# Gate and up as seven half-size block products, down in one pass per third, in a two-layer decoder kernel

## What is computed

```
def finish(x, m, w_o, g_post_mix, g_pre_ffn, g_post_ffn, w_gate, w_up, w_down):
    x = x + rmsnorm(m @ w_o, g_post_mix)
    h = rmsnorm(x, g_pre_ffn)
    f = (jax.nn.silu(h @ w_gate) * (h @ w_up)) @ w_down
    return x + rmsnorm(f, g_post_ffn)
```

## Time and profile before

| | us |
|---|---|
| runs, median (lowest to highest) | 3083.09 (3079.55 to 3083.16) |
| span of the profiled execution | 3082.5 |
| PE busy in it | 3010.5 (98%) |
| DVE, ACT, POOL busy | 1414.9, 1054.6, 759.0 (46%, 34%, 25%) |
| mean DMA rate | 85 GB/s |

### The profile page before, as it was taken

The page is one execution under the profiler, slowest core; times in us unless marked ns, Lnnn a source line. Parts: engine busy times, 40 slices in busy tenths (PEclk is TensorE's granted clock), DMA queues, the critical chain, the costliest instruction groups (busy, mean ns, idle before and its releaser), DMA issues. The chain is left out here.

```text
span 3082.5 us, 48879 instructions
## 1 busy us (share of the span) xinstructions
PE 3010.5 (98%) x19766; PEld 2637.1 (86%) x19766; DVE 1414.9 (46%) x3330; ACT 1054.6 (34%) x2094; POOL 759.0 (25%) x546
## 2 busy tenths in 40 slices
PE   8999999999999999999999999999999999999998
PEld 6777766679999999999977777665899999999997
DVE  5579675466512112122565887654584111111125
ACT  4376535564311111011333665355642111110112
POOL 3002031324312122243500201312352122121132
PEclk9999999999999999999999999999999999999999
DMA  5120335651211111121321112457311111111131
GB/s 187 32 64 28 111 112 179 235 192 52 67 45 46 48 48 42 48 66 56 117 78 47 47 35 91 160 186 244 135 59 60 48 49 48 42 48 49 43 117 57
DMA packets 254072, 263.55 MB, mean 85 GB/s; under 512 B 24993, under 2 KB 224570, under 8 KB 253850
## 3 DMA queue, kind: packets, MB, share of 16 engines
q1 hardware_dynamic: 233370, 189.11, 19.6%
q0 software_dynamic: 20480, 71.32, 6.7%
HBM read 229.73 MB, written 30.65 MB: 84 GB/s over the span
## 5 line engine op out<-in xcount | busy, mean ns | idle before, releaser
L2231 PE MATMUL ps<-act_lo,w_hi 128*128 128x352 f32 x2112 | 683.5, 324 | 5.5 <-DVE act_lo L2698 3.8
L2231 PE MATMUL ps<-act_hi,w_hi 128*128 128x352 f32 x2112 | 677.1, 321 | 0.0
L2231 PE MATMUL ps<-act_hi,w_lo 128*128 128x352 f32 x2112 | 676.8, 320 | 0.0
L2608 POOL TENSOR_TENSOR w_lo<-w_raw,w_hi 128x1024 fp32r<-128x1024 f32 x132 | 322.0, 2441 | 1024.3 <-ACT w_hi L2449 1024.2
L740 PE MATMUL ps<-w_in_slots,hT 128*128 128x256 f32 (+1 forms) x2048 | 447.6, 374 | 4.9 <-PEq L206 3.2
L740 PEld LDWEIGHTS ps<-w_in_slots,hT 128*128 128x128 f32 x2048 | 373.5, 192 | 60.8 <-issue 10.6
L2231 PEld LDWEIGHTS ps<-act_lo,w_hi 128*128 128x128 f32 x2112 | 396.2, 188 | 11.1 <-DVE act_lo L2698 5.9
L2231 PEld LDWEIGHTS ps<-act_hi,w_hi 128*128 128x128 f32 x2112 | 396.9, 188 | 0.2
L2711 DVE TENSOR_TENSOR a_raw<-ps,silu 128x352 f32<-128x352 f32 x120 | 62.9, 524 | 726.7 <-PE ps L2231 726.6
L2231 PEld LDWEIGHTS ps<-act_hi,w_lo 128*128 128x128 f32 x2112 | 396.0, 187 | 0.0
L2231 PE MATMUL ps<-a_lo,w_hi 128*128 128x352 f32 x1056 | 344.0, 326 | 0.0
(11 more groups left out here) (371 smaller groups left out, 4271.7 us busy)
## 6 DMA issues: line engine op xcount, KB each, us to landing
w_raw<-in_w_gate SPq DMA_DIRECT2D x44, 512.0 KB, 3.8
w_raw<-in_w_up SPq DMA_DIRECT2D x44, 512.0 KB, 3.8
w_raw<-in_w_down SPq DMA_DIRECT2D x44, 512.0 KB, 3.8
w_in_slots<-in_w_in SPq DMA_DIRECT2D x18, 1024.0 KB, 5.3
xpark<-xT SPq DMA_DIRECT2D x9, 1408.0 KB, 5.6
xT<-xpark SPq DMA_DIRECT2D x6, 1408.0 KB, 14.4
hT<-xpark SPq DMA_DIRECT2D x6, 1408.0 KB, 12.8
wo_raw<-in_w_o SPq DMA_DIRECT2D x16, 512.0 KB, 5.3
```

Of the source, the lines that this page charges most:

```text
L2231: ins = pe.matmul(bank(b), w, x, start=first and i == 0, stop=end and i == 2)
L2608: pool.tensor_tensor(w_lo[slot(j)][:, 0:K, :], w_raw[slot(j)][:, 0:K, :], w_hi[slot(j)][:, 0:K, :].bitcast(F32), ALU.subtract).then_inc(w_ ...
```

## The change

`seq` keeps the first 12 units (chunks 0 and 1). The other 20 chunks are taken in 10 pairs (chunk 2 + p with chunk 12 + p). For a pair, gate is one matrix product of h (T tokens by 1024 features) with a 1024 x 256 block of weights, and up another. Both are cut in halves in all three directions: 528 tokens, 4 feature blocks, 128 outputs. The 2 x 2 x 2 block product that takes eight half-size products is made of seven, from sums and differences of the blocks.

- The sums of h (`combs`: s1, s5, s2, s7, s6, each 128 x 2112) are made and split once in a layer, by DVE and ACT, and one lo by POOL. s7 and s6 lie in xT. So h is written into xT in place, after x has been copied to DRAM (`parked[th]`).
- The sums of weights are made for every product: DVE adds or subtracts (`sum_weight`, 5 of 7), ACT rounds (`round_weight`), POOL takes the rest (`rest_of_weight`), each on 128 x 512. There are four buffers (NT = 4).
- A product (`product`) is 24 matmuls of 264 columns: 12 in one bank, then 12 in the next. Per group of seven, ACT copies three results out (`keep_product`), POOL adds twice on 128 x 528 (w_34, t2), and DVE adds and multiplies (`finish_pair`, 4 instructions for a gate group, 8 for an up group).
- a goes to DRAM (`apark`) as it is made.
- Down is then 24 units (three thirds by 8 output blocks) of 22 * 3 = 66 matmuls of 352 columns, each accumulated in one bank. The weights of down are loaded and split anew for every third, in three groups (8, 6 and 8 chunks deep, `GROUPS`), two buffers. a of each third is read back through a ring of NX = 12 and split.

The diff, cut to its core:

```
+        c.apark = nc.dram_tensor("apark", (P, FC * T), F32, kind="Internal").ap()
...
+    HT = T // 2
+    QT = HT // 2
+    HK = KC // 2
...
+    A11, A12, A21, A22 = xT[:, K1, T1], xT[:, K2, T1], xT[:, K1, T2], xT[:, K2, T2]
+    combs = {"s1": (A11, A22, ALU.add), "s5": (A11, A12, ALU.add), "s2": (A21, A22, ALU.add), "s7": (A12, A22, ALU.subtract),
+             "s6": (A21, A11, ALU.subtract)}
...
+    operand = [(act_hi[:, K1, T1], act_lo[:, K1, T1]), (act_hi[:, K2, T2], act_lo[:, K2, T2])] + \
+              [(comb_hi[n], comb_lo[n]) for n in ("s1", "s5", "s2", "s7", "s6")]
...
+    PAIRS = (FC - 2) // 2
+    NQ = 2 * PAIRS
+    NP = 7 * NQ
+    f_of = lambda pair, i: 2 + pair + PAIRS * i
...
+    pair_bank = [0, 2, 4, 0, 2, 4, 6]
...
+        b11, b21, b12, b22 = f1[:, K1, :], f1[:, K2, :], f2[:, K1, :], f2[:, K2, :]
+        return ((b12, b22, ALU.subtract), (b21, b11, ALU.subtract), (b11, b22, ALU.add), (b22,), (b11,), (b21, b22, ALU.add), (b11, b12, ALU.add))[pos]
...
+    order = [0, 1] + [f_of(pair, i) for pair in range(PAIRS) for i in range(2)]
+    NX = 12
...
+    GROUPS = ((0, 8), (8, 14), (14, 22))
...
-    PART = KC
-    parts = [list(range(a, min(a + PART, FC))) for a in range(0, FC, PART)]
...
-    seq = [(j, th) for ths in ((0, 1), (2,)) for j in range(NPRE) for th in ths] + [(j, th) for j in range(NPRE, NB) for th in range(3)]
...
+    seq = [(j, th) for ths in ((0, 1), (2,)) for j in range(NPRE) for th in ths]
...
+            def load_pair(q):
+                if q >= 2:
+                    sp.wait_ge(t_lo_done, 7 * (q - 1))
+                for i in range(2):
+                    f = f_of(q // 2, i)
+                    sp.dma_start(w2[q % 2][i][:, :, :], (wu if q % 2 else wg)[:, :, f * P:(f + 1) * P]).then_inc(w2_in[q % 2], 16)
...
+            def load_a(x):
+                th, i = divmod(x, FC)
+                if i < 2:
+                    for n in range(3):
+                        sp.wait_ge(first_out[n], 32)
+                elif th == 0:
+                    sp.wait_ge(a_out[0 if (i - 2) % 2 else 2], 16 * ((i - 2) // 2 + 1))
+                if x >= NX:
+                    sp.wait_ge(d_lo_done, x - NX + 1)
+                sp.dma_start(x_ring[:, x % NX, :], apark[:, order[i], of(th)]).then_inc(x_ring_in[x // 2 % (NX // 2)], 16)
...
+            def load_down(u, g):
+                if u >= 2:
+                    sp.wait_ge(w_used, 3 * (u - 2) + g + 1)
+                a, b = GROUPS[g]
...
-            sp.wait_ge(h_lo, KC + 3)
+                sp.dma_start(third(xpark, th), third(xT, th)).then_inc(parked[th], 16)
+            sp.wait_ge(m_root, 4)
             load(1)
...
+            def bank_free(q, pos):
+                if q == 0:
+                    for b in (pair_bank[pos], pair_bank[pos] + 1):
+                        n = max(x for x in range(len(seq)) if unit_bank(x) == b)
+                        pe.wait_ge(mul if up(n) else sg_done, nth[n])
+                elif pos < 2:
+                    pe.wait_ge(silu_done if q % 2 else a_mul, 4 * ((q - 1) // 2) + pos + 1)
+                else:
+                    pe.wait_ge(post, 4 * (q - 1) + (3 if pos == 2 else 4))
+
+            def product(q, pos):
+                m = 7 * q + pos
+                e, b = m % NT, pair_bank[pos]
+                x_hi, x_lo = operand[pos]
+                opens, closes = pos in (0, 1, 2, 6), pos >= 3
+                pe.wait_ge(t_lo_done, m + 1)
+                if opens:
+                    bank_free(q, pos)
+                else:
+                    pe.wait_ge(kept, 3 * q + pos - 2)
+                if q == 0 and pos == 3:
+                    pe.wait_ge(s5_lo_done, 1)
+                elif q == 0 and pos >= 2:
+                    pe.wait_ge(comb_lo_done, max(1, pos - 2))
+                for h in range(2):
+                    for k in range(HK):
+                        for i, (w, x) in enumerate(((t_hi[e], x_lo), (t_hi[e], x_hi), (t_lo[e], x_hi))):
+                            ins = pe.matmul(ps[:, b + h, 0:QT], w[:, k, :], x[:, k, h * QT:(h + 1) * QT], start=opens and k == 0 and i == 0,
+                                            stop=closes and k == HK - 1 and i == 2, skip_group_check=True)
+                ins.then_inc(p_mm, 1)
+
+            for q in range(NQ):
+                for pos in range(7):
...
+            for u in range(NU):
+                th, d = divmod(u, KC)
+                b = u % 6
+                if u < 6:
+                    pe.wait_ge(a_mul if b < 4 else post, 4 * PAIRS - 3 + b // 2 if b < 4 else 4 * NQ - 1)
+                else:
+                    pe.wait_ge(y_done, u - 5)
+                for i in range(FC):
+                    g = group_of[i]
+                    a, end = GROUPS[g]
+                    if i == a:
+                        if g < 2:
+                            pe.wait_ge(wd_lo_pool, wd_pool_nth[u, g])
+                        else:
...
+                dve.wait_ge(parked[th], 32 if th == 2 else 16)
                 for k in range(KC + 1):
...
+            def sum_weight(m):
+                e, src = m % NT, weight(m)
+                if len(src) == 1:
+                    return
+                dve.wait_ge(w2_in[m // 7 % 2], 32 * (m // 14 + 1))
+                if m >= NT:
+                    dve.wait_ge(p_mm, m - NT + 1)
+                dve.tensor_tensor(t_raw[e][:, :, :], *src).then_inc(t_sum, 1)
+
+            def finish_pair(q, pos):
+                pair, gate, which = q // 2, q % 2 == 0, pos - 3
+                dve.wait_ge(p_mm, 7 * q + pos + 1)
+                if pos == 3:
+                    dve.wait_ge(w_34_done, q + 1)
+                    if pair:
+                        dve.wait_ge(silu_done if gate else a_out[2], 4 * (pair - 1) + 3 if gate else 16 * pair)
+                    dve.tensor_tensor(flat(t1[q % 2]), flat(w_34), S, ALU.subtract).then_inc(post, 1)
+                elif pos == 4:
+                    dve.wait_ge(t2_done, q + 1)
+                    if pair:
...
+            for u in range(4):
+                multiply_up(u)
+            sum_comb("s1")
+            sum_weight(0)
+            sum_weight(1)
+            dve.wait_ge(mm, 9)
+            sum_weight(2)
+            sum_comb("s5")
+            multiply_up(4)
+            rest_of_comb("s1")
+            dve.wait_ge(mm, 11)
+            sum_comb("s2")
+            multiply_up(5)
+            sum_comb("s7")
+            sum_comb("s6")
+            rest_of_comb("s2")
+            tail = {NP - 3: range(4), NP - 2: range(4, 8), NP - 1: range(8, 11)}
+            for done in range(1, NP + 1):
+                q, pos = divmod(done - 1, 7)
+                if done + 3 < NP:
+                    sum_weight(done + 3)
+                if done == 2:
+                    rest_of_comb("s7")
+                if done == 3:
+                    rest_of_comb("s6")
+                if pos >= 3:
+                    finish_pair(q, pos)
+                if done == NP - 3:
+                    dve.wait_ge(t2_done, NQ)
+                if done in tail:
+                    rest_of_a(0, *tail[done])
+            rest_of_a(0, 11)
+            rest_of_down(0)
```

746 lines of the change are left out of this document (466 added, 280 removed).

## The result

The changed kernel takes **3034.97 us** (median of 4 runs, 3033.54 to 3035.31), beside 3083.12 us for the kernel before on the same chip (3079.55 to 3083.29). The ratio is 0.9846, with a 95% interval of 0.9832 to 0.986. So it is 48 us faster, where 64 were forecast; 3035 lies in the range of 2980 to 3080.

A forecast was written before the change was run, and what follows sets the result against it. PE was taken to bound the kernel, by number of matmuls and distance between them. The sum 3082.5 - 94.0 + 2 * 10 + 2 * 1.5 + 2 * 3 + 1 = 3018.5 gave 3019 us, range 2980 to 3080.

The forecast's parts named there:

- Part 1: Gate and up of 20 chunks: 264-column matmuls 0.1223 us apart, a gain of 47.0 us a layer, 94.0 in both.
- rival 2: Products: the excess is a shared limit on columns and weights together, 0.130 us a matmul, about 3070 us; chance 0.13.
- rival 3: Products: the weight side sets the distance whatever the width, 0.159 us a matmul, 3265 us; chance 0.10.
- Rival 5: Products: no excess at 264 columns, 0.1125 us a matmul, 2953 us; chance 0.04.
- Part 2: Products, steady part: DVE, ACT and POOL can feed PE's 20.5 us a group of seven; waits taken as 0.
- rival 4: Products: the weight chain DVE, ACT, POOL takes 10.3 us, longer than three products; 70 us a layer, 3159 us; chance 0.06.
- The factor of 2.5: Earlier trace: a DVE row growing from 0.51 to 1.27 us while POOL adds, cited for rival 4.
- Part 3: Start of the products: PE waits for DVE, ACT and POOL, 10 us a layer, plus 1.5 of half clock.
- up to 4 in which POOL shuts DVE out: Start of the products: up to 4 us added to DVE's 15.6 us list ahead of the sixth `a_raw`.
- The hand-over: From the last products to down: PE waits 0 to 5 us for DVE's chain, taken as 3 a layer.
- Down: Down's units: pace unchanged, weights and a fed in time; POOL's gathers cost 1 us once.
- Parking x: Writing h into xT: DVE's wait until x is parked costs 0, or 1 us at most.

The follow-up runs named there:

- e6: The changed kernel with its product matmuls taking 200 of their 264 columns, the others left out; 0.1117 us between matmuls.
- e9: The changed kernel with the products of groups 4 to 19 taking 128 of their 264 columns, groups 0 to 3 whole; 3018 us.
- e5: The changed kernel with reordered lists at the products' start, s5's rest on DVE, SP's hand-over order changed and reads of x spread; 3011.08 us, ratio 0.9777.
- e12: e5 plus sixth a_raw ahead of s1's rest, unit 1's weights later, ACT's second and third product copies ahead of rounding s7 and s6; 3006.24 us.
- e3: The changed kernel with SP issuing reads of a's chunks 12 and up ahead of waits for the last products and unit 1's weights; ratio 0.9833.
- e4: The changed kernel with the three reads of x spread over units 3, 5 and 11 of down instead of together in unit 2; ratio 0.9831.
- e2: The changed kernel with the rest of s5 taken by DVE behind the sixth a_raw, not by POOL; ratio 0.9865.

## Why the prediction was right, and where it was off

**Part 1, the pace, was right.** The distance of 0.1223 us was off by 0.0007: 0.1216 in the stretch. The excess that each matmul carries is nearly the same at 264 columns as at 352, 0.0116 us against 0.0126. Why it is there, which the prediction put down to the overlap of a weight load with each matmul, no run tested. There are 824 matmuls in 100 us, where 818 were forecast, 770 for rival 2 and 630 for rival 3; both fall. Rival 5 falls too: 0.1125 is not reached at 264 columns; e6 and e9 reach about that only at 200 and 128. The prediction read 0.115 as the pace of the weight loads from the earlier trace rows; the floor measured is 0.1117. So 264 columns lie above it, with 0.0099 us to spare. As an estimate from this, a matmul of 132 columns would save only these 0.0099 us, so a second halving would not pay.

**Part 2 was right.** In 380 us PE never waits, so rival 4 falls. POOL is busy 60% of 100 us, as the 12.2 of 20.5 us said. DVE's price was too low: a weight sum took 1.19 us on average where 0.69 was taken (0.69 for the 46 of 200 that no POOL instruction overlaps, 1.34 for the other 154), but PE had room for it. The factor of 2.5 that the prediction read from the earlier trace rows compared two different instructions; the slower one takes 0.58 us (median) in that profile and 1.27 beside POOL, a factor of 2.2.

**Part 3, the start, was right in kind and short by 2.7 us a layer.** Product 2 waits for the sixth `a_raw`, ended by DVE, as said. But the wait is 7.5 us and not 0 to 4, and the fifth product's 3 to 12 did not come. The sixth `a_raw` came 23.2 us after h, and not 15.6 to 19.6. Two terms were short. One is "up to 4 in which POOL shuts DVE out", which was 5: POOL's rest of s5 was counted against products 5 and later, and it lay in front of product 2 (6.78 instead of 2.35 us for one sum). The other is DVE's list, which was added up as if DVE had to wait for nothing but one DMA, and which stood 2.44 us for PE's fifth up unit. That the total of 10 came so near (11.2 between starts) is in part luck: the wait ahead of product 2 was 3.5 us over its bound, and the one ahead of product 5 didn't come. In part it has a reason that e5 and e12 speak for: the waits there follow from the length of a shared queue, and an order mostly changes where they fall. The half clock cost 3.0 and not 1.5 us, near the upper bound of 3.2.

**The hand-over was mis-sized: 9.7 us a layer where 3 was taken and 5 was the bound.** The sum counted DVE's instructions and POOL's 6.8 us in their way, and that part did show: two of the five waits fall beside POOL. What failed is that it took ACT to have a in time: SP's list put the reads of chunks 12 and up behind waits for the last products and behind 1.4 MB of weights, and ACT stood for 5.54 us. e3 gives 3 us of it back by SP's order alone. The 2.5 us of half clock behind it was not counted either. This is the largest part of the miss, 13.4 of 15 us.

**Down was mis-sized: 2.5 + 1.4 us a layer, where 1 once was taken.** The prediction compared the mean, 190 GB/s with 399. It didn't look at what is issued at one time. Behind three reads of 1408 KB the weights for units 3 and 4 took up to 11 us to land, where 3.3 is usual (e4). The pace of down is 0.0009 us a matmul worse, with DMA at 0.5 to 0.9 of its time; whether that is the cause wasn't tested.

**Parking x was right** at about nothing; PE's wait in the units grew by 0.7 us, for POOL's `w_lo` and not for the parking. **The end** is as before: 19.3 us from the last sum over y to the end in both.

Three gains weren't foreseen: 1.7 us in layer 0 and 0.3 in layer 1 in the sums over y (by difference only), 2.1 in the mixing stage and 1.8 in the output projection of layer 1. The change touches neither of the last two; in each one stretch of half clock is missing. Whether that has to do with the change wasn't shown, so some 4 of the 49 us may be no gain of it.

The version e12 beats both kernels: 3006.2 us, ratio 0.9758 to the kernel before, and 0.9758 / 0.9846 = 0.991 to the changed one.

## What to carry to other kernels

To price a matmul of a new width, take the distance between starts from a stretch where PE is never idle, keep the excess over the columns as it is, and set a floor at the shortest distance that any width shows (here 0.1117 us): a block product with fewer and narrower matmuls pays only above it. Where a stage begins with much work for DVE and POOL, add up what both do there as one queue before reordering anything. Here reordering, with one step moved from POOL to DVE, took the products from 421.6 to 416.1 us, and from there on it only moved the wait; PE alone would need 408.6. At a hand-over follow SP's list in order, with every wait in it, and look at what is issued at once, not at the mean rate.

## What the runs showed of the hardware

- The granted clock held either of its two levels for one stream of matmuls. With 128 columns and a weight load each, PE stayed at half clock for 720 us once it had fallen in a wait of 7.75 us, and at full clock for all of groups 4 to 19 where it had begun there. The kernels took 3621.8 and 3018.1 us, though the second has four whole groups in each layer and thus more work. In e6, with 200 columns, a wait of 7.73 us was followed by 10 us at half clock and then by the full clock. So one wait can cost far more than its own length.
- Float32r matmuls with 128x128 weights of their own start 0.1117 us apart at full clock, at 200 columns as at 128. At 128 columns and half clock they start 0.213 us apart.
- At half clock the distance at 264 columns is 0.220 us, the columns at 1.2 GHz and nothing beside, as at 352 before (0.293).
- A DVE sum of 128x2112 took 2.35 us where POOL was idle, 3.41 beside the last part of a POOL instruction, and 6.78 beside one of 6.75 us (e2 and the changed kernel). Of DVE's 200 weight sums on 128x512 in the changed kernel, the 46 that no POOL instruction overlaps took 0.69 us each; the other 154 took 1.34 on average, and none of them less than 1.0.
- Three DMAs of 1408 KB in a row made the next six issues on the same queue take 1.4 to 3.8 us instead of 0.5.
